# Interleaved first chunk in eleven blocks, a norm by Ln and Exp, and narrower clearing of PSUM banks

## What is computed

```python
# even: stick-breaking and sparse attention; fox: attention with forget gates
x = x + mixer(rmsnorm(x, g), w_in, ...)                       # even, fox, dilated
# conv0, conv1
a, b = split(rmsnorm(x, g) @ w_in); a = causal_conv3(a) + conv_b
x = x + (silu(a) * b) @ w_out
# glu0..glu3
gate, up = split(rmsnorm(x, g) @ w_in); x = x + 0.5 * (silu(gate) * up) @ w_out
# hgrn: a gated linear recurrence o, and then, for each head of width 128
o = rms(o, out_gain) * silu(g);  x = x + o @ w_out            # rms: o * rsqrt(mean(o*o) + 1e-6) * gain
# kv: keys and values of one rmsnorm(x), shared by the attention of dilated
```

## Time and profile before

| | |
|---|---|
| time, three runs | 2018.73 us median (2012.76 to 2021.49) |
| the profiled execution | 2011.54 us |
| its span | 2009.6 us, granted TensorE clock 0.991 |
| TensorE busy | 1925.9 us, 96% |
| VectorE, ScalarE, GpSimd busy | 60%, 49%, 6% |
| DMA | 320.56 MB, 160 GB/s in the mean |

### The profile page before, as it was taken

How to read it: one execution, slowest core, us unless ns; L and a number is a source line. 1 busy time by engine, 2 the same in 40 slices (tenths; PEclk the granted TensorE clock), 3 DMA queues, 4 the chain that set the end, 5 groups by cost and what they waited for, 6 DMA issues and landing times.

```text
span 2009.6 us, 36835 instructions
## 1 busy us (share of the span) xinstructions
PE 1925.9 (96%) x15867; PEld 1841.9 (92%) x15867; DVE 1212.1 (60%) x1406; ACT 975.6 (49%) x1153; POOL 119.2 (6%) x54
## 2 busy tenths in 40 slices
PE   7999999999999999999989999999999998899998
PEld 7979999898999999999979999899999986779998
DVE  6677666656766775567657555433555565646554
ACT  5465443555434544444335334777534456644342
POOL 0000000010000000000000000333000011220000
PEclk9999999999999999999989999999999999999999
DMA  6314544443455455544325555454455536435552
GB/s 257 127 43 173 188 183 160 164 145 106 168 188 188 147 174 187 186 152 166 106 85 186 178 182 188 145 176 156 167 182 188 184 136 184 107 100 177 185 188 84
DMA packets 57568, 320.56 MB, mean 160 GB/s; under 512 B 5950, under 2 KB 19509, under 8 KB 20213
## 3 DMA queue, kind: packets, MB, share of 16 engines
q1 hardware_dynamic: 55700, 313.93, 45.2%
q10 hardware_dynamic: 1760, 5.07, 0.7%
HBM read 317.85 MB, written 1.12 MB: 159 GB/s over the span
## 4 chain that ended last, share of the span: by engine, by line
PE 81%; DVE 10%; ACT 5%; issue 2%; DMA 1%; SPq 0%; ACTq 0%; DVEq 0%
PE bank L373 25%; PE bank L375 24%; PE bank L374 24%; DVE lo L346 3%; ACT hi L340 2%; DVE xl L894 1%; PE bank L438 1%; DVE x L907 1%; PE bank L475 1%; PE bank L1829 1%; DVE arena L1931 1%; DVE arena L531 1%; PE bank L456 0%; ACT xh L1008 0%; PE bank L2231 0%
## 5 line engine op out<-in xcount | busy, mean ns | idle before, releaser
L373 PE MATMUL bank<-xh,hi 128*128 128x256 f32 x2960 | 849.1, 287 | 21.4 <-DVE xl L894 18.6
L374 PE MATMUL bank<-xl,hi 128*128 128x256 f32 x2960 | 839.9, 284 | 0.0
L375 PE MATMUL bank<-xh,lo 128*128 128x256 f32 x2960 | 839.6, 284 | 0.0
L346 DVE TENSOR_TENSOR lo<-ring,hi 128x2048 fp32r<-128x2048 f32 x273 | 621.5, 2280 | 314.1 <-ACT hi L340 313.3
L340 ACT ACTIVATE hi<-ring 128x2048 fp32r<-128x2048 f32 x291 | 551.8, 1899 | 434.9 <-PE bank L375 428.8
L373 PEld LDWEIGHTS bank<-xh,hi 128*128 128x128 f32 x2960 | 568.8, 192 | 36.9 <-issue 19.2
L374 PEld LDWEIGHTS bank<-xl,hi 128*128 128x128 f32 x2960 | 569.0, 192 | 1.7 <-issue 1.5
L375 PEld LDWEIGHTS bank<-xh,lo 128*128 128x128 f32 x2960 | 568.9, 192 | 0.3
L373 PE MATMUL bank<-gh,hi 128*128 128x256 f32 x1056 | 300.1, 284 | 7.2 <-DVE gl L824 7.2
L374 PE MATMUL bank<-gl,hi 128*128 128x256 f32 x1056 | 299.5, 284 | 0.0
L375 PE MATMUL bank<-gh,lo 128*128 128x256 f32 x1056 | 299.5, 284 | 0.0
(11 more groups left out here) (272 smaller groups left out, 1972.6 us busy)
## 6 DMA issues: line engine op xcount, KB each, us to landing
ring<-in_ffn_in SPq DMA_DIRECT2D x132, 1024.0 KB, 4.9
ring<-in_ffn_out SPq DMA_DIRECT2D x66, 1024.0 KB, 4.8
ring<-in_kv SPq DMA_DIRECT2D x24, 1024.0 KB, 4.9
ring<-in_hg_in SPq DMA_DIRECT2D x16, 1024.0 KB, 4.8
ring<-in_od_in SPq DMA_DIRECT2D x12, 1024.0 KB, 4.9
ring<-in_dq SPq DMA_DIRECT2D x12, 1024.0 KB, 4.9
ring<-in_ev_in SPq DMA_DIRECT2D x11, 1024.0 KB, 5.0
arena<-rel_rows SPq DMA_DIRECT2D x24, 256.0 KB, 3.7
```

The lines of the kernel that those rows point to most:

```text
L346: ns.tensor_tensor(lo[n % RING][:, 0:w], ring[n % RING][:, 0:w], hi[n % RING][:, 0:w].bitcast(F32), ALU.subtract).then_inc(lo_ok[lo_by[n]], 1)
L373: nc.tensor.matmul(out_, lh, rh, start=start, stop=False, **kw)
L374: nc.tensor.matmul(out_, lh, rl, start=False, stop=False, **kw)
L375: return nc.tensor.matmul(out_, ll, rh, start=False, stop=stop, **kw)
```

## The change

`pe_together` runs several halves side by side: for each pair of k-tiles it waits once and then does that pair for every half. Blocks even, hgrn, kv and dilated do this with the two halves of their first chunk; conv and glu blocks with these and the first half of the second chunk; fox with its first chunk (16 columns wide) and the first half of its second. Only the first half of a bank opens it (start flag); the other adds onto cleared flags. In hgrn Sqrt and `reciprocal` are replaced by Ln and Exp with scale -0.5. The clearing matmuls write 4 columns instead of 512. In the last step of a conv or glu block the low split of the next block's first chunk moves from ahead of the taps to behind `gl`. A helper that nothing calls (`make_head_norm`) goes.

```diff
+        def pe_together(pe, halves, first):
+            for n, B, h, width, opens in halves:
+                if h == 0:
+                    wait_split(pe, n)
+            for i in range(4):
+                pe.wait_ge(xg_new, first + i + 1)
+                for n, B, h, width, opens in halves:
+                    wh, wl = slot(n, width, hi), slot(n, width, lo)
+                    m = min(P, width - h * P)
+                    e = slice(h * P, h * P + m)
+                    for k in (2 * i, 2 * i + 1):
+                        last = product(B[0:m, h * T:(h + 1) * T], wh[:, k, e], wl[:, k, e], xh[:, k, :], xl[:, k, :],
+                                       opens and k == 0, k == KT - 1, skip_group_check=True)
+                    if i == 3 and (h == 1 or width <= P):
+                        last.then_inc(chunk_mul, 1)
+
+        def pe_first_chunk(pe, b, B):
+            n = info[b]["c0"]
+            pe_together(pe, [(n, B, 0, CW, True), (n, B, 1, CW, False)], first_xg(b))
...
         def pe_part_of(pe, n, B, h, ks, tiles, acts, order=tuple(range(KT))):
...
-                nc.tensor.matmul(B[:, :], zero16[:, :], zero16[:, :].unsqueeze(1).broadcast_to([1, 4, P]), start=True,
-                                 stop=False, skip_group_check=True)
+                nc.tensor.matmul(B[:, 0:4], zero16[:, :], zero16[:, 0:4], start=True, stop=False, skip_group_check=True)
...
         def ff_in(pe, j, par, n, F, first, it=None):
             if first is None:
                 pe.wait_ge(ff_read, 2 * (F + j))
-            for h in range(2):
-                wait_split(pe, n + h, it)
+            else:
+                pe_together(pe, [(n, bank[2 * par], e, CW, e == 0) for e in range(2)] + [(n + 1, bank[2 * par + 1], 0, CW, True)],
+                            first)
+            for h in range(0 if first is None else 1, 2):
+                if first is None:
+                    wait_split(pe, n + h, it)
                 wh, wl = slot(n + h, of=hi), slot(n + h, of=lo)
                 B = bank[2 * par + h]
-                for e in range(2):
+                for e in range(0 if first is None else 1, 2):
...
         def dve_ff_step(dve, b, j, par, F, first, conv, it=None):
...
-                lo_until(dve, m + (3 if first else 4))
+                lo_until(dve, m + (3 if first or par == 0 else 4))
...
         # fox, pe_part
-                for c in range(4):
-                    if c == 2:
-                        pe_stats(pe, "fox")
-                    pe_chunk(pe, n0 + c, bank[c], "tm" if c == 3 else "fm", 16 if c == 0 else CW,
-                             first_xg("fox") if c == 0 else None)
+                pe_together(pe, [(n0, bank[0], 0, 16, True), (n0 + 1, bank[1], 0, CW, True)], first_xg("fox"))
+                pe_half(pe, n0 + 1, bank[1], "fm", 1)
+                pe_stats(pe, "fox")
+                pe_chunk(pe, n0 + 2, bank[2], "fm")
+                pe_chunk(pe, n0 + 3, bank[3], "tm")
...
         # hgrn
-                nc.scalar.activation(RN[:, 2 * (p % 2):2 * (p % 2) + 2, :], halves(bank[mean_bank[p]]), ACT.Sqrt,
+                nc.scalar.activation(RN[:, 2 * (p % 2):2 * (p % 2) + 2, :], halves(bank[mean_bank[p]]), ACT.Ln,
                                      bias=eps_c[:, :]).then_inc(o_rn, 1)
+            def act_inverse(act, p):
+                act.wait_ge(o_rn, p + 1)
+                two = slice(2 * (p % 2), 2 * (p % 2) + 2)
+                nc.scalar.activation(RN[:, two, :], RN[:, two, :], ACT.Exp, scale=-0.5).then_inc(o_ex, 1)
 
             def dve_norm(dve, p):
                 two = slice(2 * (p % 2), 2 * (p % 2) + 2)
-                dve.wait_ge(o_rn, p + 1)
-                nc.vector.reciprocal(RN[:, two, :], RN[:, two, :]).then_inc(o_n, 1)
-                dve.wait_ge(o_n, 2 * p + 1)
+                dve.wait_ge(o_ex, p + 1)
                 nc.vector.scalar_tensor_tensor(OT[:, two, :], halves(out_bank(p)), vecs[:, ROW_OUT_GAIN:ROW_OUT_GAIN + 1],
                                                RN[:, two, :], ALU.mult, ALU.mult).then_inc(o_n, 1)
...
                     if i in (11, 12):
                         act_root(act, i - 11)
+                    if i == 12:
+                        act_inverse(act, 0)
+                        act_inverse(act, 1)
...
                 act_root(act, 2)
                 act_root(act, 3)
+                act_inverse(act, 2)
+                act_inverse(act, 3)
                 hi_until(act, n0 + 18)
```

More of the change, by code:

```diff
@@ L663, in pe_stats, with pe_half @@
                                  stop=True).then_inc(fin_stat, 1)
-        def pe_half(pe, n, B, mode, h, width=CW, first=None, tiles=None, acts=None, freed=False, ks=range(KT)):
+        def pe_half(pe, n, B, mode, h, width=CW, tiles=None, acts=None, freed=False, ks=range(KT)):
             if h == 0 and 0 in ks:
@@ L688, in pe_half, with pe_chunk @@
                 last.then_inc(chunk_mul, 1)
-        def pe_chunk(pe, n, B, mode, width=CW, first=None, tiles=None, freed=False):
+        def pe_chunk(pe, n, B, mode, width=CW, tiles=None, freed=False):
             for h in range(1 if mode == "fm" and width <= P else 2):
-                pe_half(pe, n, B, mode, h, width, first, tiles, freed=freed)
+                pe_half(pe, n, B, mode, h, width, tiles, freed=freed)
+        def pe_together(pe, halves, first):
[16 more added lines that the diff above has]
+            pe_together(pe, [(n, B, 0, CW, True), (n, B, 1, CW, False)], first_xg(b))
         def pe_part_of(pe, n, B, h, ks, tiles, acts, order=tuple(range(KT))):
@@ L764, in pe_ffn @@
                     pe.wait_ge(std_new, info[b]["st"])
-                nc.tensor.matmul(bank[y][:, :], zero16[:, :], zero16[:, :].unsqueeze(1).broadcast_to([1, 4, P]), start=True, stop=False,
+                nc.tensor.matmul(bank[y][:, 0:4], zero16[:, :], zero16[:, 0:4], start=True, stop=False,
                                  skip_group_check=True)
@@ L1432, in pe_part @@
             def pe_part(pe):
-                pe_chunk(pe, n0, bank[0], "fm", first=first_xg("even"))
+                pe_first_chunk(pe, "even", bank[0])
                 pe_stats(pe, "even")
@@ L1970, in pe_part @@
                         pe.wait_ge(*of_chunk(c - 3))
-                    pe_chunk(pe, n0 + c, chunk_bank(c), "fm", first=first_xg("hgrn") if c == 0 else None)
+                    if c == 0:
+                        pe_first_chunk(pe, "hgrn", chunk_bank(0))
+                    else:
+                        pe_chunk(pe, n0 + c, chunk_bank(c), "fm")
                 for i in range(20):
@@ L2132, in turned_round @@
             return v.rearrange("p e (a b) -> p e a b", a=2)[:, :, :, ::-1]
[L2134 to L2192, removed]
-                act.dma_start(consts, A["consts_" + tag]).then_inc(const_in, 16)
-                for c in range(12):
-                    hi_until(act, n0 + c + 2)
-                    act.wait_ge(s["lin"], c + 1)
-                    if c >= 2:
-                        act.wait_ge(s["mean"], c - 1)
-                    nc.scalar.activation(tmp_sq[c % 2], dst[:, 2 * c:2 * c + 2, :], ACT.Square).then_inc(s["sqr"], 1)
-                    if c >= 2 and c % 2 == 0:
-                        act_norm(act, c - 2)
-            return s, mean, pe_part, dve_part, act_part, dve_norm, act_norm
@@ L2234, in pe_part @@
                     early = value and k > 0
-                    for h in range(2):
+                    if c == 0:
+                        pe_first_chunk(pe, "kv", bank[0])
+                    for h in range(2 if c else 0):
                         if h and early:
                             mean()
-                        pe_half(pe, n0 + c, bank[c % 4], "tm" if value else "fm", h, first=first_xg("kv") if c == 0 else None,
-                                freed=c == 23)
+                        pe_half(pe, n0 + c, bank[c % 4], "tm" if value else "fm", h, freed=c == 23)
                     if c == 0:
@@ L2376, in run @@
                             pe.wait_ge(*soft.at("pt", 12))
-                    pe_half(pe, n0 + c, bank_of(c), "fm", h, first=first_xg("dilated") if c == 0 else None)
+                    pe_half(pe, n0 + c, bank_of(c), "fm", h)
                 return run
@@ L2494, in pe_part @@
             def pe_part(pe):
-                project(pe, 0)
+                pe_first_chunk(pe, "dilated", bank_of(0))
                 pe_stats(pe, "dilated")
```

8 lines of the change are left out of this document (2 added, 6 removed).

## The result

The changed kernel takes 1992.76 us in the median of four runs (1987.09 to 1997.33), the kernel before 2015.74 beside it (2011.49 to 2021.49): ratio 0.988 with a 95% interval of 0.984 to 0.9925. The forecast was 1993. The profiled execution of the changed kernel is its slowest, 1997.33 with a span of 1995.4 and a granted clock of 0.987; that of the kernel before is near its fastest, 2011.54 (span 2009.6, 0.991). So the two traces lie 14.2 us apart and the medians 23.0.

A forecast was written before the change was run, and what follows sets the result against it. TensorE sets the end, so its waits can be won: boundaries 11.9, norm 10.5 and clearing 3.0 sum to 25.4 us, taking the profiled 2011.54 to 1986.1 and the median from 2018.73 to 1993; range 1983 to 2006.

The forecast's parts named there:

- four gate starts: Starts of conv0, conv1, glu1, glu3: interleaving wins 1.1 us each, though a new 1.1 wait for the second split appears; 4.4.
- fox: Start of fox: interleaving gains 1.6 us, and the narrow split leaving the path of `gl` 0.2; together 1.8.
- hgrn start: Start of hgrn: with interleaving the first chunk ends at 899.2 instead of 900.8, a gain of 1.6 us.
- kv: Start of kv: the wait moves ahead of the statistics (1.5), but ScalarE's root comes 1.0 earlier; gain 0.9 us.
- dilated: Start of dilated: as in kv, the wait moves ahead of the statistics and root waits shrink; gain 1.0 us.
- conv1's end and final norm: Moved split: `gl` ends about 3 us earlier in conv1, but VectorE's chain limits the final-norm block's gain to 2.2.
- HGRN level products: Heads' pairs 0 and 1: without reciprocals TensorE's two waits go, 5.5 us, and low-clock matmuls behind them, 1.2 more.
- HGRN output product: Pairs 2 and 3: TensorE goes on at 1042.3 instead of 1046.11, 3.8 us, despite a new 2.3 wait.
- narrow clearing: Gate blocks and output parts: 21 of the clearings count, each saving 0.15 us; 3.0 in all.
- Rival (c): Switching between halves costs, about 100 switches; at 0.35 us each 10 slower, median 2029; chance 0.04.
- rival (a): Block boundaries give back what they win, bringing 3 us instead of 11.9; median 2002; chance 0.22.
- rival (b): More goes than counted: Exp shares Ln's table, clearings cost nothing, later waits shrink; 33 us, 1985; chance 0.12.

The follow-up runs named there:

- the late wait: Against the changed kernel: interleaved starts wait for the second chunk's low split only behind the first chunk's first pair of k-tiles; 1993.43 us, 0.9877 to the kernel before.
- The repeat: The changed kernel run once more, unchanged, for a second trace; 1996.74 us, ratio 0.9884 to the kernel before.
- the kernel with ScalarE's order changed: Against the changed kernel: the high split of HGRN's third output chunk stands ahead of the last two Exp on ScalarE; 1991.24 us, 0.9873 to the kernel before.
- the combined kernel: Changed kernel plus late second-split wait, high split ahead of last two Exp, low split deferred in fox and final-norm block; 1984.09 us, 0.9839 to the kernel before.

## Why the prediction was right, and where its sizes were off

The segments between fixed instructions of TensorE (so the first product of a block, the first one behind its statistics) give a size for each step. They repeat to about 0.02 us between traces wherever no slow matmuls and no late load lie in them.

```
step                            predicted   measured in the changed kernel's trace
four gate starts                   4.4      1.1 + 1.1 + 1.1 + 1.2 = 4.5
fox                                1.8      1.7 + 0.2 - 0.9 = 1.0
hgrn start                         1.6      1.6
kv                                 0.9      1.0
dilated                            1.0      -3.3 (interleaving alone: 1.2)
conv1's end and final norm         2.2      3.0 + 0.3 + 0.7 - 1.4 = 2.6
HGRN level products                6.7      1.4 + 3.9 + 1.4 = 6.7
HGRN output product                3.8      6.3 + 1.8 - 2.3 = 5.7
narrow clearing                    3.0      1.1 here, up to 2.4 with what lies inside other rows
```

*The waits for `xl` are filled.* Right in place and size at the gate starts and hgrn. No gap shows where halves switch: conv1's 96 matmuls take 11.59, 0.121 each. (The change makes 112 switches, since six gate blocks have 12 each, and not 100.) Rival (c) is out. Of rival (a), that the boundaries give back, fox and dilated came true; of rival (b), that more goes, the output product did.

*The starts wait for the second split.* Right: 0.93 in conv1 where 1.1 was said. Had the wait stood behind the first pair of halves, it would have cost nothing, as the late wait shows; the prediction took the code as it was.

*Kv and dilated move their wait to the statistics.* Right in kv: 1.4 ahead of the statistics, 1.5 predicted, and undoing it costs nothing measurable in time. Dilated's gain is there when interleaving is made alone (1.2). In the changed kernel it is not: its three traces take 3.3, 2.1 and 1.5 longer there than the kernel before. In the first a load of the ring landed 1.4 later and 10 slow matmuls followed, with 16 more ahead of it, behind the wait for the first `xl`; why the load came later isn't settled.

Part of this goes with the moved split, which lengthens the wait ahead of the first product of kv and of dilated from 0.9 to 1.75. In nine of the ten traces of kernels with the moved split, 11 to 16 matmuls in a row ran 0.21 apart within 10 us behind one of these waits or both; in the four traces without it none did. Where such a stretch lies ahead of the statistics, the wait there (1.4) takes it up, but in kv the root then comes about 0.8 later (14.87 instead of 14.10 from the first product, 15.01 before). The prediction named no such cost for the move. No run takes the move alone out of the changed kernel, so that it is the cause is likely and not shown.

*The moved split.* Right: `gl` gains 3.0, the final-norm chain gives part back as a longer wait ahead of the third clearing, 3.7 (4.5 predicted). The 2.2 of the sum stands against 2.6 up to the product behind the clearings, of which 0.2 belongs to these. For glu0, glu1 and glu2 the forecast was no gain; the traces show 0.8 won at `gl` and 0.75 to 0.8 lost at the next start. This is the case in which one must not add what a wait loses: taken alone the move is worth nothing that the interval can tell. Beside the interleaving glu0's start falls by 0.7 instead of growing by 1.0, and that too comes to nothing: from conv1's last step to the third clearing it is 26.06 in the changed kernel and 26.07 with the move alone, against 28.45 before, since the clearing waits for VectorE's chain (3.69 instead of 1.68).

*Fox, mis-sized.* Two low splits (4.49 together) now stand ahead of the reciprocal of the statistics on VectorE, since the statistics come 1.6 earlier and the splits don't:

```profile
374.83 4.49 DVE L346 TENSOR_TENSOR lo<-ring,hi 128x2048 fp32r<-128x2048 f32 x2
...
379.24 0.16 DVE L983 RECIPROCAL rs_c<-std_c 128x2 f32<-128x2 f32 x1
```

Everything up to `cum_r` is 0.9 late by it. The prediction asked what waits for the first chunk, and not what stands ahead of the statistics' own chain; deferring one split gave 0.6 of it back.

*Norm.* The level products are right to the tenth between these two traces. (Of the four other traces with the old norm one takes as long there as the kernel before and three take 0.7 to 1.0 more, with more slow matmuls; so the tenth is luck.) For the output product I had added a low-clock stretch of 1.6 behind the new wait. It did not come in the changed kernel's traces, and so this term is 5.7 and not 3.8, of which 0.4 is the narrow clearing of two chunks ahead; the stretch came with the norm alone, where the term is 4.0. The wait was 2.3 long there and 2.69 here, and behind 2.69 in the kernel with the late wait the stretch came again. The table load ahead of Exp is there. By the Trainium skill, "ScalarE: Activation LUTs", section "Table sets: the hidden batching unit", Ln and Exp share a set and the second load would be absent; the trace shows 1.28 at 1024.68, and the measurement decides.

*Clearing, mis-sized.* Clearings stand 0.02 to 0.04 apart, and each could save 0.2, more than the 0.15 assumed (21 of them at 0.15 are 3.15, not 3.0). But in conv0, conv1, glu1 and glu3 the last one hangs on ScalarE's root, and the product stays 0.30 behind it, so each of these wins 0.02. In glu2 the four together win 0.78, in the final-norm block 0.24, in an output part 0.21 each, where no wait behind it takes it back.

**Why 14 in the traces and 23 in the medians.** The steps that the table shows won add up to 24.2 without dilated. The changed kernel's trace loses 10.0 of it: 1.4 since the input x landed later ahead of the first block, 3.8 by low-clock stretches in `even`, whose code around them did not change, 1.5 by one after fox's wait, and 3.3 in dilated. The granted clock tells of it: 0.987 against 0.991, with 118 slow matmuls against 89. The repeat has the same stretches in `even`, the kernel with ScalarE's order changed has not: its span is 1985.4, with 0.992. So the profiled execution of before fell on the good side and that of after on the bad one; the forecast by the ratio of the medians hit, and the four runs of each are spread over 10 us; those of the changed kernel go with their granted clock (0.987, 0.988, 0.990 and 0.992 from the slowest to the fastest).

That the forecast lies 0.3 us beside the median is luck, and its mechanism does not need it. The steps without dilated were forecast at 24.4 and measured at 24.2 only because errors cancel: fox 0.8 and the clearings 1.9 too high, the output product 1.9 and the final norm 0.4 too low. The 25.4 of the sum stands against 14.2 between the traces. And it was scaled to a median before of 2018.73; with the 2015.74 measured beside the changed kernel the same sum gives 1990.

**What stays open.** The parts, each alone in the kernel before, add up to 0.0069 of the time; the whole change gives 0.0114 to 0.0117 in its three measurements. The norm within the change is worth 13.2 us against 9.7 alone, though the kernel before has medians of 2014.5 and 2017.3 beside them. In the traces 1.7 of this lies in the output product (4.0 with the norm alone, 5.7 in the changed kernel), mostly the slow stretch. Where the rest lies isn't shown; at glu0's start, where one would look for it, the third clearing stands at the same distance with and without the interleaving. The intervals of the four parts leave 2 to 3 us each.

## What to carry to other kernels

Where a consumer waits for arrivals one by one, give each arrival enough work (here 18 matmuls, 2.15 us, for arrivals 1.4 apart), and make each wait stand directly ahead of the first instruction that needs it, not ahead of the whole group. When a step gets earlier, look at what stands in the queues ahead of the chain that follows it: fox's reciprocal behind two splits, HGRN's split behind two inverses and the final-norm chain behind two splits cost 0.6, 2.45 and 1.1 us. Reordering these three and waiting later at the four gate starts (3.5) made the combined kernel 10.6 us faster than the change. Size such edits by segments of the trace, since edits of a few us are lost in runs that lie 10 apart.

## What the runs showed of the hardware that was not expected

The same wait is followed by half clock in one execution and not in another. Here the windows behind the wait of 2.69 ahead of the third output chunk, of the changed kernel and of the one with the late wait, which differ in nothing near it; the columns are the window, its length, the busy times of five engines with their counts, the granted clock, the DMA share and GB/s:

```profile
1031.40:1033.40 2.00, 1.99 (x17) 1.97 (x18) 1.88 (x3) 0.63 (x1) 0.00 (x0) 1.00 0.58 111
```

```profile
1029.00:1031.00 2.00, 2.00 (x10) 1.98 (x11) 1.86 (x4) 0.64 (x1) 0.00 (x0) 0.50 0.55 115
```

In the first TensorE ran at 2.4 GHz, in the second at 1.2, and 10 matmuls fit where 17 did. Six traces have this wait at 2.69 to 2.70, and only this one has a slow stretch behind it; the norm alone, with a wait of 2.29, has one of 15. Most stretches comprise 8 to 27 matmuls, 0.21 apart instead of 0.12: 0.8 to 2.5 us. A trace holds 88 to 165 such matmuls, 8 to 15.5 us, and the two traces with 88 and 89 are of different kernels. With their cost taken off, the span is 2001.3 before, 1984.3 after and 1982.4 in its repeat: 17 to 19 us apart, which is nearer to the medians than the spans are. The span of a single trace of this kernel carries that cost, which lies anywhere in 7 us, though its segments repeat to hundredths.
